# Six stage changes of a two block kernel, taken by token tile

## What is computed

```python
h = swiglu(rms_norm(x, ff1_norm_pre), w_gate, w_up, w_down)     # ff1
x = x + 0.5 * rms_norm(h, ff1_norm_post)
h = hybrid_mixer(rms_norm(x, mix_norm_pre), ...)                # mix_in, attention, mix_out
x = x + rms_norm(h, mix_norm_post)
h = swiglu(rms_norm(x, ff2_norm_pre), ...)                      # ff2
x = x + 0.5 * rms_norm(h, ff2_norm_post)
x = x + attention(rms_norm(x, mixer_norm[0]))                   # att_in, attention, att_out
x = x + conv_glu_ffn(rms_norm(x, ffn_norm[0]), ...)             # glu1
x = x + gated_delta_net(rms_norm(x, mixer_norm[1]))             # gdn_qkv, gdn_z, gdn_out
x = x + conv_glu_ffn(rms_norm(x, ffn_norm[1]), ...)             # glu2
```

## Time and profile before

| | |
|---|---|
| median of three runs | 1408.58 us (1407.69 to 1408.87) |
| the profiled execution | 1410.13 us, its span 1408.1 us |
| PE busy | 1356.0 us, 96% of the span |
| DVE busy | 922.3 us, 65% |
| ACT busy | 669.2 us, 48% |
| POOL busy | 98.4 us, 7% |
| mean granted TensorE clock | 0.991 of full speed |

### The profile page before, as it was taken

One profiled execution on the slowest core, in us unless ns is written; L12 is line 12 of the kernel. 1 busy time (PEld: TensorE's weight loads), 2 busy tenths in 40 slices (PEclk: granted clock), 3 DMA queues, 4 the chain that ended last, 5 costly groups with the idle time before them and its releaser, 6 DMA issues.

```text
span 1408.1 us, 24387 instructions
## 1 busy us (share of the span) xinstructions
PE 1356.0 (96%) x9818; PEld 1246.0 (88%) x9830; DVE 922.3 (65%) x1378; ACT 669.2 (48%) x983; POOL 98.4 (7%) x93
## 2 busy tenths in 40 slices
PE   5999999998999999998999999999999999999998
PEld 5999988987789999797799999799999887999997
DVE  5655565766465555677566666679988874766665
ACT  5444344545443443456444444457642553544443
POOL 1000000000000000020000000003300540000000
PEclk9999999998999999999999999999999999999999
DMA  7655553640145555350255555434432124455551
GB/s 265 212 185 192 187 179 119 226 150 1 60 165 180 183 191 192 120 180 31 90 180 179 179 183 193 161 126 171 154 127 84 35 78 159 161 189 192 191 192 61
DMA packets 30311, 214.82 MB, mean 153 GB/s; under 512 B 3488, under 2 KB 3616, under 8 KB 4768
## 3 DMA queue, kind: packets, MB, share of 16 engines
q1 hardware_dynamic: 29808, 212.23, 43.8%
q0 software_dynamic: 432, 1.57, 0.3%
HBM read 212.74 MB, written 1.05 MB: 152 GB/s over the span
## 4 chain that ended last, share of the span: by engine, by line
PE 83%; DVE 10%; ACT 3%; issue 2%; POOL 1%; DMA 1%; SPq 0%; DVEq 0%; POOLq 0%; ACTq 0%
PE bank L457 73%; DVE w_lo L1780 2%; PE bank L652 2%; ACT w_hi L1191 1%; POOL stat L1639 1%; PE bank L665 1%; PE bank L696 1%; DVE arena L2178 1%; DVE par L2176 1%; DVE xn L1813 1%; PE bank L1068 1%; ACT aT_hi L1209 1%; DMA pos_i<-positions 1%; PE bank L950 0%; DVE stat L2008 0%
## 5 line engine op out<-in xcount | busy, mean ns | idle before, releaser
L1780 DVE TENSOR_TENSOR w_lo<-raw,w_hi 128x2048 fp32r<-128x2048 f32 x199 | 458.9, 2306 | 207.5 <-ACT w_hi L1191 207.1
L457 PE MATMUL bank<-aT_hi,w_hi 128*128 128x256 f32 x1728 | 491.1, 284 | 5.5 <-DVE aT_lo L1801 4.9
L457 PE MATMUL bank<-aT_hi,w_lo 128*128 128x256 f32 x1728 | 488.9, 283 | 0.0
L457 PE MATMUL bank<-aT_lo,w_hi 128*128 128x256 f32 x1728 | 488.9, 283 | 0.0
L1191 ACT ACTIVATE w_hi<-raw 128x2048 fp32r<-128x2048 f32 x199 | 380.1, 1911 | 118.8 <-PE bank L457 116.7
L457 PEld LDWEIGHTS bank<-aT_hi,w_hi 128*128 128x128 f32 x1728 | 331.3, 192 | 10.9 <-DVE w_lo L1780 8.1
L457 PEld LDWEIGHTS bank<-aT_lo,w_hi 128*128 128x128 f32 x1728 | 331.4, 192 | 1.5
L457 PEld LDWEIGHTS bank<-aT_hi,w_lo 128*128 128x128 f32 x1728 | 331.4, 192 | 0.0
L457 PE MATMUL bank<-w_hi,hT_hi 128*128 128x512 f32 (+1 forms) x432 | 166.1, 384 | 1.9 <-DVE hT_lo L1897 1.9
L457 PE MATMUL bank<-w_hi,hT_lo 128*128 128x512 f32 (+1 forms) x432 | 165.6, 383 | 0.0
L457 PE MATMUL bank<-w_lo,hT_hi 128*128 128x512 f32 (+1 forms) x432 | 165.3, 383 | 0.0
(11 more groups left out here) (327 smaller groups left out, 1357.2 us busy)
## 6 DMA issues: line engine op xcount, KB each, us to landing
raw<-weights SPq DMA_DIRECT2D x199, 1024.0 KB, 4.9
post_gain<-post_gains POOLq DMA_DIRECT2D x3, 512.0 KB, 4.2
residual<-x SPq DMA_DIRECT2D x2, 512.0 KB, 4.0
out<-residual SPq DMA_DIRECT2D x2, 512.0 KB, 2.6
par<-params SPq DMA_DIRECT2D x1, 837.0 KB, 7.5
con<-consts SPq DMA_DIRECT2D x1, 520.0 KB, 10.7
con<-consts SPq DMA_DIRECT2D x1, 64.0 KB, 6.0
pos_i<-positions SPq DMA_DIRECT2D x1, 1.0 KB, 7.3
```

The lines of the kernel that those rows point to most:

```text
L457: last = nc.tensor.matmul(to, lhsT, rhs, start=start and n == 0, stop=stop and n == 2)
L1780: nc.vector.tensor_tensor(w_lo[:, i % 3, :], raw[:, i % 3, :], w_hi[:, i % 3, :].bitcast(f32), ALU.subtract).then_inc(w_lo_done, 1)
```

## The change

It does the same at all six stage changes, by token tile.

- **Last products per tile.** `project_out` does both last items for t = 0, signals (`y_done`), and then both for t = 1. In `ff1`, `ff2`, `glu1` the last two `down` do t = 0 of the first, t = 0 of the last (signal), t = 1 of the first, t = 1 of the last. For this the `split` in the chain of the last tile moves behind `hT_hi` and `hT_lo`, and the `split` of the item behind the first of the two moves into the stage change.
- **Raw rows turned** into `mix_in` and `att_in`: PE transposes x itself, not scaled rows, and the row factor (`row_rstd`) is applied when the products are copied out of PSUM (`copy_block`: two copies of 256 columns in place of one of 512). In the other four the rows are scaled as before (`scale_rows`).
- **Per tile** is also the post norm (DVE now multiplies the result by the gain while POOL takes the root, and then does scale and add in one instruction), the transposes (`turn_half`), `aT_hi` and `aT_lo` (16 of 128x128 in place of 8 of 128x256 on each engine). Tile 0 goes into banks 0, 1, 6, 7 and tile 1 into 2, 3, 0, 1.
- **First items by tile.** `mix_in`, `att_in`: t = 0 of items 0, 1, transposes of tile 1, t = 0 of item 2, and then t = 1 of items 0, 1, 2. Feed-forward stages: t = 0 of tile 0, transposes of tile 1, t = 0 of tile 1, t = 1 of tile 0, t = 1 of tile 1; `gdn_qkv` likewise. In these the weights stay stationary and 128 token columns move in place of 256, with twice as many matmuls and weight loads.
- **No unused products**: `keep_clock` is gone.
- `ffn_order` writes out two pairs more of `glu1` in place of one more turn of its loop.

```diff
-            def keep_clock(to, n):
-                for _ in range(n):
-                    nc.tensor.matmul(to[:, :], ident, con[:, 0:512], start=True, stop=True)
...
+            def turn_half(name, t):                       # PE
+                if name in RAW_POWERS:
+                    pe.wait_ge(x_ready, 2 * NORMS.index(name) + t - 1)
+                else:
+                    pe.wait_ge(rows_ready, 2 * SCALED_ROWS.index(name) + t + 1)
+                for k in range(8):
+                    rows = x if name in RAW_POWERS else xn
+                    last = nc.tensor.transpose(half_bank(t, k), rows[:, t, 128 * k:128 * k + 128], ident)
+                    if k % 2:
+                        last.then_inc(half_turned, 1)
...
+                def tile_rows(f, i, t):
+                    pe.wait_ge(w_lo_done, i + 1)
+                    for part in range(2):
+                        for k in range(8):
+                            at = 1024 * part + 128 * k
+                            if f == 0 and part == 0 and k % 2 == 0:
+                                pe.wait_ge(half_lo, halves(name, t, k) + 1)
+                            cols = slice(256 * part + 128 * t, 256 * part + 128 * t + 128)
+                            last = exact(bank[4 + f][:, cols], weights(i, at, at + 128),
+                                         left(k, 128 * t, 128 * t + 128), k == 0, k == 7)
+                    return last
...
                 def tile(f, i, q):
+                    if name in HALVED and f == 0:
+                        turn_half(name, 0)
+                        pe.wait_ge(hid_ready, f0 - 2)
+                        tile_rows(0, i, 0)
+                        turn_half(name, 1)
+                        tile_rows(1, i + 1, 0)
+                        tile_rows(0, i, 1).then_inc(item_done, 1)
+                        return
+                    if name in HALVED and f == 1:
+                        tile_rows(1, i, 1).then_inc(item_done, 1)
+                        return
...
+                    final = m == n_tiles // 2 - 1
+                    last = down_rows(m, i, 0)
+                    if final:
+                        last.then_inc(y_done, 1)
+                    if name in BEHIND and m == n_tiles // 2 - 2:
+                        return
+                    if name in BEHIND and final:
+                        down_rows(m - 1, i - 1, 1).then_inc(item_done, 1)
+                    down_rows(m, i, 1).then_inc(item_done, 1)
...
+                part_rows(1, parts - 2, 0)
+                part_rows(1, parts - 1, 0).then_inc(y_done, 1)
+                part_rows(1, parts - 2, 1).then_inc(item_done, 1)
+                part_rows(1, parts - 1, 1).then_inc(item_done, 1)
...
+            def first_rows(name):                         # PE, mix_in and att_in
+                turn_half(name, 0)
+                project_early(name, 0, 0)
+                project_early(name, 1, 0)
+                turn_half(name, 1)
+                project_early(name, 2, 0)
...
+            def into_halves(result, name):                # ACT, into mix_in and att_in
+                post_squares(result, (0,))
+                split(FIRST[name] + 1)
+                turn_half(name, 0)
+                post_squares(result, (1,))
+                split(FIRST[name] + 2)
+                turn_half(name, 1)
+                row_squares(name, 0)
+                row_squares(name, 1)
...
+            def scale_rows(name, t):                      # DVE
+                dve.wait_ge(squares_ready, 2 * n + t + 1)
+                power_of(nc.vector.tensor_scalar(rstd[:, t:t + 1], sumsq[:, t:t + 1], 1.0 / D, EPS, ALU.mult, ALU.add))
+                nc.vector.tensor_scalar(xn[:, t, :], x[:, t, :], rstd[:, t:t + 1], None, ALU.mult).then_inc(rows_ready, 1)
...
+            def normed_halves(name, norm, factor):        # DVE, into ff2
+                add_normed(norm, factor, 0)
+                split(FIRST[name] + 1)
+                scale_rows(name, 0)
+                root = scale_results(norm, factor, 1)
+                turn_half(name, 0)
+                add_scaled(norm, 1, root)
+                scale_rows(name, 1)
+                turn_half(name, 1)
+                split(FIRST[name] + 2)
...
+            def plain_halves(result, name):               # DVE, into glu1, gdn_qkv, glu2
+                dve.wait_ge(y_done, RESULTS.index(result) + 1)
+                ...                                       # x of tile 0 += banks 0, 1
+                if result not in BEHIND:
+                    nc.vector.tensor_tensor(x[:, 1, 0:512], x[:, 1, 0:512], bank[2][:, :], ALU.add)
+                scale_rows(name, 0)
+                split(FIRST[name] + 1)
+                dve.wait_ge(item_done, end)
+                ...                                       # x of tile 1 += what is left of banks 2, 3
+                turn_half(name, 0)
+                scale_rows(name, 1)
+                turn_half(name, 1)
+                split(FIRST[name] + 2)
...
+            def into_halves(name, norm, factor):          # DVE, into mix_in and att_in
+                add_normed(norm, factor, 0)
+                split(FIRST[name] + 1)
+                turn_half(name, 0)
+                add_normed(norm, factor, 1)
+                split(FIRST[name] + 2)
+                turn_half(name, 1)
```

More of the change, by code:

```diff
@@ L48 @@
 FFNS = {"ff1": (22, False, 0), "ff2": (22, False, 22), "glu1": (24, True, 44), "glu2": (24, True, 68)}
-TURNS = ["ff1", "mix_in", "mix_out", "ff2", "att_in", "att_out", "glu1", "gdn_qkv", "gdn_out0", "gdn_out1", "glu2"]
+TURNS = ["ff1", "mix_out", "att_out", "gdn_out0", "gdn_out1"]
 NORMS = ["ff1", "mix_in", "ff2", "att_in", "glu1", "gdn_qkv", "glu2"]
+BEHIND = {"ff1": "mix_in", "ff2": "att_in", "glu1": "gdn_qkv"}
+HALVED = ["mix_in", "ff2", "att_in", "glu1", "gdn_qkv", "glu2"]
+SCALED_ROWS = ["ff1", "ff2", "glu1", "gdn_qkv", "glu2"]
+RAW_POWERS = {"mix_in": 6, "att_in": 16}
 RESULTS = ["ff1", "mix_out", "ff2", "att_out", "glu1", "gdn_out", "glu2"]
@@ L576, in project_out @@
                 parts = 2 * halves
-                for h in range(2):
[L578 to L604, removed]
@@ L911, in convolved @@
                     last.then_inc(item_done, 1)
+                turn_half("gdn_qkv", 0)
+                channel_rows(0, 0)
+                turn_half("gdn_qkv", 1)
+                channel_rows(1, 0)
+                for k in range(16):
+                    if k < 2:
+                        channel_rows(k, 1).then_inc(item_done, 1)
+                    else:
+                        channels(k)
                     if k == 0:
@@ new lines, in copy_block @@
+            def copy_block(layer, i, n, block):
+                act.wait_ge(item_done, i + 1)
+                act.wait_ge(rstd_ready, RAW_POWERS[layer])
+                for t in range(2):
+                    last = nc.scalar.activation(proj[:, t, 256 * block:256 * block + 256],
+                                                bank[4 + n % 3][:, 256 * t:256 * t + 256], ACT.Copy,
+                                                scale=row_rstd[:, t:t + 1])
+                last.then_inc(copied, 1)
@@ L1579, in _ @@
             ffn("ff1")
-            post_squares("ff1")
-            pre_norm("mix_in")
+            into_halves("ff1", "mix_in")
             mixer_projection()
@@ L1592, in _ @@
             turn_out("att_out", lambda k: 1.0)
-            splits(FIRST["att_out"], 3)
+            splits(FIRST["att_out"], 2)
+            plain_halves("glu1")
             ffn("glu1")
-            pre_norm("gdn_qkv")
+            plain_halves("gdn_qkv")
             convolved()
@@ L1816, in pre_norm @@
                     split(0)
-                if name in ("ff2", "glu1", "glu2"):
-                    split(FIRST[name] + 1)
                 turn_out(name, lambda k: gains[:, n, k:k + 1])
@@ new lines, in turn_half @@
+            def turn_half(name, t):
+                n = NORMS.index(name)
+                for k in range(8):
+                    if k % 2 == 0:
+                        dve.wait_ge(half_hi, halves(name, t, k) + 1)
+                    rows = slice(128 * t, 128 * t + 128)
+                    last = nc.vector.scalar_tensor_tensor(aT_lo[:, k, rows], half_bank(t, k), gains[:, n, k:k + 1],
+                                                          aT_hi[:, k, rows].bitcast(f32), ALU.mult, ALU.subtract)
+                    if k % 2:
+                        last.then_inc(half_lo, 1)
@@ L2405, in _ @@
             ffn("ff1")
[L2406 to L2407 removed]
+            into_halves("mix_in", 0, 0.5)
             mixer_projection()
```

280 lines of the change are left out of this document (186 added, 94 removed).

## The result

| | before | after |
|---|---|---|
| median of the runs | 1408.13 us (4 runs, 1407.31 to 1408.87) | 1466.87 us (4 runs, 1463.42 to 1470.26) |
| ratio, after / before | | 1.0417, 95% interval 1.0383 to 1.0451 |
| profiled execution, its span | 1410.13, 1408.1 us | 1463.42, 1461.6 us |
| mean granted clock | 0.991 | 0.959 |

The change costs 4.2%, 53.5 us of span. The direction was forecast, the size was not: 1427 us, with 1443 as the upper end. Of the four runs after, two took 1463.4 and 1463.6 us at a mean granted clock of 0.959, and two took 1470.1 and 1470.3 us at 0.953; the profile is of the first of them.

The account below looks back on a forecast made before the run. PE, busy in 96% of the span, was taken as the bound, with 56.5 us of stage-change windows to win. Stage terms gave +10.5, with the clock +18.5: 1428.6 us profiled, 1427 us median, range 1404 to 1443.

Parts of the forecast that it names:

- five falls, 8.0 us: Without `keep_clock`, clock falls into `ff2`, `glu1`, `gdn_qkv`, `glu2` and at the end of `glu1`, 1.6 us each.
- three more falls: Upper end of the range: further clock falls, +5 us, with halves at 0.125 us (+11.5), giving 1443 us.
- The price of half a product: An fp32r matmul of 128 moving columns, bound by its weight load: 0.110 us, ends 0.106 and 0.125.
- The rivals with 0.067, 0.081 and 0.214 us: Other prices per half: stream rate, 1396 us, chance 0.07; page's figure, 1406 us, 0.08; plain float32, 1507 us, 0.06.
- The starts: PE's waits without products into the six stages: 2.3 `mix_in`, `att_in`; 5.6 `ff2`; 3.1 `glu1`, `glu2`; 4.3 us `gdn_qkv`.
- The two good stages: `mix_in` and `att_in`, where the token tile is stationary and splitting costs nothing: -7.2 and -4.7 us.
- The four halved stages: Stages with 128 moving columns get longer: `ff2` +4.3, `glu1` +6.0, `gdn_qkv` +6.1, `glu2` +6.0 us.
- The end of `glu1`: PE still stands 1.8 us for `hT_lo`; without a clock fall it would end at 905.5, not 907.3.
- No fall into `mix_in` and `att_in`: Stretches of 2.3 and 1.7 us with transposes in them; no clock fall counted (two to three more would be 5).
- One reading of the trace before: One stretch where PE stood 1.9 us without `keep_clock`, then half clock: 1.6 us lost, taken as a fall's price.
- the fast rival: Halves at the rate of the stream, 0.067 us a matmul: 1396 us, chance 0.07.
- halves as dear as plain float32: Two records per half in the four split stages, 0.214 us: about +98, 1507 us, chance 0.06.

Follow-up runs that it names:

- second experiment: The changed kernel with unused products put back in PE's gaps at four stage changes, halves kept: 1424.91 us, ratio 1.0106 to the kernel before.
- the first: The kernel before with both calls of `keep_clock` removed, so long gaps stand ahead of products of 256 columns: 1421.70 us, ratio 1.0079.
- third experiment: The changed kernel with first items of `ff2`, `glu1`, `gdn_qkv`, `glu2` whole (256 columns moving), no unused products: 1401.35 us, ratio 0.9945.
- the last experiment: The changed kernel with whole first items, unused products in the gaps, both tiles' rows made ahead of the two splits: 1392.53 us, ratio 0.9892.
- fourth experiment: The kernel before, unused products kept, with the first two items of `ff2`, `glu1`, `gdn_qkv`, `glu2` in halves of 128 columns: 1469.95 us, ratio 1.0469.
- fifth experiment: The kernel before, unused products kept, with later items of the four stages in halves, behind products of 256 columns: 1468.26 us, ratio 1.0432.
- the first six experiments: All runs listed here but the last experiment, plus the changed kernel with five unused 512-column products behind the first 48 halves of four stages: 1461.07 us.

## Why the prediction was wrong in size

Each stage is taken from PE's last product of the stage before to its own last. "Clock" is half of the time that the four stretches above (and 2.4 us behind the first) ran low.

| us | forecast without clock | measured | clock | measured less clock |
|---|---|---|---|---|
| `ff1` | 0 | +0.1 | | +0.1 |
| `mix_in` and attention | -7.2 | -9.7 | | -9.7 |
| `ff2` | +4.3 | +25.3 | 22.4 | +2.9 |
| `att_in` | -4.7 | -5.5 | | -5.5 |
| `glu1` | +6.0 - 1.8 | +8.8 | 5.1 | +3.7 |
| `gdn_qkv` and behind | +6.1 + 1.8 | +21.9 | 15.4 | +6.5 |
| `glu2` | +6.0 | +12.6 | 6.9 | +5.7 |
| sum | +10.5 | +53.5 | 49.8 | +3.7 |

- **The step that failed is the last term of the sum, "five falls, 8.0 us".** Four falls cost 49.8 us. (Half is a little too much: halves start 0.2138 us apart in place of 0.1118, which is 48%. The second experiment gives another reckoning. Its span, without the four falls, is 40.2 us shorter than that of the kernel after, with 13.6 us more at the low clock in other places, 6.8 lost: together 47.) Four of the five places were right; the price was read from the earlier trace rows, where products of 512 columns ran behind the fall. The row was true and stood for another shape: behind 256 columns a fall costs about as little (the first and third experiments), behind halves it cost 5 to 22 us, and in `ff2` and `gdn_qkv` it lasted until products of 256 columns ran. The prediction had halves and a fall side by side and did not ask what the clock does with halves behind a fall, a case of which the trace before has no row. Its range took in three more falls, and none of them longer.
- **The price of half a product was right**: 0.110 us forecast (0.106 to 0.125), 0.1118 measured over 353 intervals in the kernel after at full clock, while 256 columns stayed at 0.1199. At 1.2 GHz it is 0.2138. The rivals with 0.067, 0.081 and 0.214 us at full clock are out. The prediction compares 107 ns for the load of 128 columns with "the row"; what agrees is the distance of starts, 106 ns, while the fp32r load itself is recorded at 192 ns. The Trainium skill (TensorE: Matmul & The Clock Gate, section on the back-to-back issue gap) gives 81 ns for 128 columns; with fp32r operands the trace doesn't agree, and the measurement decides.
- **The starts were right**: 2.3, 5.6, 2.3, 3.1, 4.3 and 3.1 us forecast, 2.44, 5.47, 2.44, 3.05, 3.65 and 3.05 measured. What was said to be next in line (the pair of `aT_lo`, and into `ff2` root and scaling) is what the chain of the kernel after shows, in order of time (start, us, what), with the `split` of the second item ahead of it, which the last experiment moves behind:

```profile
372.69 2.29 DVE w_lo L1946
...
375.13 0.57 POOL stat L1804
...
376.73 1.20 DVE xn L2002 x2
377.92 0.61 DVE aT_lo L2064 x2
...
378.67 1.51 PE bank L474 x6
```

- **The two good stages** came out 2.5 and 0.8 us better than forecast. In `mix_in` part of it is other than the change: attention has falls of the clock of its own in every kernel here, and in this execution they were shorter (the same stage took 174.4 us, not 176.8, in the fourth and fifth experiments, which don't touch it). In `att_in` it went the other way, 6.8 us at the low clock in attention against 3.4 before.
- **The four halved stages**, less the clock, cost +2.9, +3.7, +6.5 and +5.7 against +4.3, +4.2, +7.9 and +6.0. Taking off the clock flatters `ff2`: at half speed PE no longer waits for tile 1. At full speed, in the second experiment, it lost 3.9.
- **The end of `glu1`**, where a fifth fall was counted: PE stood 1.38 us in place of 1.89, and the clock held. `glu1` ended 2.1 us better for it; the forecast had 1.8 and set a fall of 1.6 against them.
- **No fall into `mix_in` and `att_in`** was right, with 2.5 us between products and eight transposes in it.
- **One reading of the trace before was too narrow.** It shows more than the one stretch behind a standstill that the prediction names: attention ran at a granted 0.50 or 0.51 from 314.1 to 321.0 us and from 338.0 to 341.4, and there are two more near 635 and 1086; and at 943 PE stood 2.06 us and the clock held. None of them has halves of fp32r behind it, so none would have given the price.
- **Two slips of addition** move nothing: the work on DVE in `att_in` adds up to 28.5 us and not 28.3, and the fast rival to -20.5 and not -20.3.

The prediction's rival on the slow side, halves as dear as plain float32, has the 0.214 us a half that the low clock shows. Its 1507 us is as far off as the forecast's 1427, 40 us, and its reason is out, for there is one record for each half, and 353 of them show 0.112. It was the clock that doubled them.

What is not settled: why the halves of `glu2` fell in the fourth experiment and those of `glu1` didn't, behind the same 1.1 us; and why the low stretches of `glu1` and `glu2` in the kernel after ended while halves were running. Both ended some 2 us behind tile 1's eight transposes, but the same transposes stand in the low stretches of `ff2` and `gdn_qkv`, which went on. No run here took the transposes away.

## What to carry to other kernels

In these runs the price of a clock fall followed what ran behind the gap more than the gap, so cost each gap with the matmul shape that follows: here a standstill into `ff2` cost 21 us of clock in halves, and 1.4 in products of 256 columns (the third experiment). Don't buy an early start with matmuls half as wide that cost nearly as much each (0.112 against 0.120 us); the start gained 6.7 us in `ff2`, the halves ate 10.6 and the clock another 20 (the first two items of the second experiment, 27.8, against 48.0). And when a change bundles a reordering with a new shape, time the reordering alone: here it was worth 8 us (1409.52 - 1401.35), and 16 with the clock covered and rows scaled first (1408.25 - 1392.53).

## What the runs showed of the hardware

- Behind a fall, a stream of fp32r products with 128 moving columns did not reliably bring TensorE's clock back from 1.2 GHz: PE issued for 42.5, 41.8 and 37.1 us without a pause at a granted 0.50, and in two other places the clock came back while halves ran, after 10.2 and 13.7 us. With products of 256 columns it was back 1.9 to 4.9 us after their first (after and the first six experiments), with five of 512 within the 6.1 us that they took in `ff2`. Once at 2.4 GHz, halves held it (192 in 21.7 us at 1.00).
- A standstill of 2.0 us or more ahead of halves was followed by a fall in 9 of 9 places, one of 1.1 us in 1 of 3. In `glu1` and `gdn_qkv` of the kernel after and in the fourth experiment the fall began 1.7, 2.3 and 2.3 us into the halves, while PE was issuing; in the fifth, with the first half. With 256 columns behind it, the standstill of 2.06 us was followed by a fall in three of eight kernels, of 3.4 to 6.8 us. The Trainium skill (TensorE: Matmul & The Clock Gate, section on HAM oscillation) tells of a kernel with few rows whose clock falls again and again, and puts that down to waits on DMA. Here the falls stand behind waits too, but for DVE (`aT_lo`, `xn`), and the long low stretches had no waits in them, DMA share 0.19 and busy PE 42.50 of 42.50 us.
- At 1.2 GHz halves and whole products start equally far apart, 0.21 us, and so a half costs as much as a whole one; at 2.4 GHz it is 0.112 against 0.120.
